# Streaming encoder: attention values held stationary in two column halves, whole key tiles

## What is computed

```
s = q @ k.T * HD**-0.5                      # fox: + c_q - c_k (running sums of a log forget value)
s = where(key allowed for query, s, -inf)   # fox: causal; dsa: chunk-causal and among the top 256 of an index score
p = softmax(s); o = p @ v                   # dsa: one k and one v for all four heads
```

## Time and profile before

| | us |
|---|---|
| median of 3 runs | 2261.97 (2259.77 to 2267.71) |
| the profiled execution's own time | 2242.35 |
| its span in the profile | 2240.4 |
| attention stage, layer 1 (from the keys' second turn to the mixers' first matmul) | 556.6 to 840.8 |
| TensorE busy in the span | 2069.9 (92%) |
| VectorE / ScalarE / GpSimd busy | 1483.6 / 641.7 / 325.3 |

### The profile page before, as it was taken

One profiled execution on the slowest core, in us unless ns is written; L12 is line 12 of the kernel. 1 busy time (PEld: TensorE's weight loads), 2 busy tenths in 40 slices (PEclk: granted clock), 3 DMA queues, 4 the chain that ended last, 5 costly groups with the idle time before them and its releaser, 6 DMA issues. The chain is left out here.

```text
span 2240.4 us, 27372 instructions
## 1 busy us (share of the span) xinstructions
PE 2069.9 (92%) x9906; PEld 1273.2 (57%) x9930; DVE 1483.6 (66%) x3125; ACT 641.7 (29%) x1478; POOL 325.3 (15%) x418
## 2 busy tenths in 40 slices
PE   3999999998999996999969999999989999979997
PEld 3644444446776775666445444444467777756663
DVE  3256999999454545877333579999975545468871
ACT  3334000101333333444143430011023333334441
POOL 0000000000000004656200000000000000146651
PEclk9999999999999996999979999999989999879999
DMA  7221132222102202233051212311130022022321
GB/s 278 81 68 35 67 118 75 75 68 72 33 8 88 81 1 104 69 104 108 38 187 53 66 67 83 108 65 59 58 80 20 6 92 76 32 74 76 118 87 59
DMA packets 144006, 169.95 MB, mean 76 GB/s; under 512 B 68560, under 2 KB 106192, under 8 KB 143600
## 3 DMA queue, kind: packets, MB, share of 16 engines
q1 hardware_dynamic: 118400, 135.52, 19.0%
q10 hardware_dynamic: 25472, 32.66, 4.1%
HBM read 115.53 MB, written 62.50 MB: 79 GB/s over the span
## 5 line engine op out<-in xcount | busy, mean ns | idle before, releaser
L767 PE MATMUL ps<-wring,xnT_arena 128*128 128x512 f32 (+3 forms) x2304 | 883.0, 540 | 0.0
L767 PEld LDWEIGHTS ps<-wring,xnT_arena 128*128 128x128 f32 x2304 | 430.7, 190 | 431.4 <-issue 369.4
L1485 DVE TENSOR_SCALAR_CACHE_REDUCE arena<-arena,theta 32x1056 bf16<-32x1056 f32 x496 | 471.5, 987 | 8.8
L1573 DVE TENSOR_REDUCE small<-ps 128x1 f32<-128x192 f32 (+9 forms) x148 | 114.0, 770 | 152.1 <-PE ps L942 145.4
L1178 ACT COPY arena<-ps 128x512 f32<-128x512 f32 (+2 forms) x96 | 51.2, 533 | 464.4 <-PE ps L767 464.4
L1470 DVE SCALAR_TENSOR_TENSOR arena<-arena,iw 128x512 f32<-128x512 f32 (+6 forms) x224 | 135.7, 606 | 57.3 <-ACT arena L1233 50.5
L1065 PEld LDWEIGHTS ps<-arena 128*128 128x128 f32 x632 | 102.6, 209 | 102.5 <-DVE arena L1673 51.7
L1065 PE MATMUL ps<-arena 128*128 128x128 f32 (+1 forms) x632 | 124.7, 330 | 38.9 <-DVE arena L1673 32.5
L1009 PE MATMUL ps<-wring,arena 128*128 128x512 f32 x320 | 152.6, 607 | 5.7 <-DVE arena L1614 5.7
L1326 ACT ACTIVATE arena<-ps,small 128x192 f32<-128x192 f32 (+9 forms) x148 | 111.0, 750 | 156.6 <-DVE small L1573 156.5
L1009 PE MATMUL ps<-wring,xnT_arena 128*128 128x512 f32 x256 | 118.3, 593 | 0.0
(11 more groups left out here) (239 smaller groups left out, 2526.0 us busy)
## 6 DMA issues: line engine op xcount, KB each, us to landing
wring<-in_w_in SPq DMA_DIRECT2D x24, 1024.0 KB, 7.6
projected<-arena ACTq DMA_DIRECT2D x96, 256.0 KB, 2.0
arena<-residual SPq DMA_DIRECT2D x36, 512.0 KB, 5.2
arena<-projected SPq DMA_DIRECT2D x36, 384.0 KB, 3.8
arena<-projected SPq DMA_DIRECT2D x18, 512.0 KB, 6.2
residual<-arena SPq DMA_DIRECT2D x18, 512.0 KB, 2.7
wring<-in_w_out SPq DMA_DIRECT2D x8, 1024.0 KB, 7.4
out<-arena SPq DMA_DIRECT2D x16, 512.0 KB, 3.9
```

The lines of the kernel that those rows point to most:

```text
L767: o = mm(bank(pbank(k), 0, wide), xnT[:, c, t * P:(t + 1) * P], w, start=(c == 0), stop=(c == CH - 1))
L1485: V.tensor_scalar(cmp_out[r, (i % 2) * WMAX:(i % 2) * WMAX + uw[u]], score[u][r], th_, 0.0, op, ALU.add, accum_out=into[r, i:i + 1]).then_ ...
L1573: V.tensor_reduce(mneg[:, s:s + 1], ps[:, base + lo:base + hi], X, ALU.max, negate=True).then_inc(a_max, 1)
```

## The change

Three things change together, all in the attention.

1. **Whole key tiles.** Key tile 0 is kept with all its 128 columns, and every piece is 128 wide and begins at a multiple of 128, scores at column 0 of the job's first bank. What has to stay hidden in tile 0 is hidden by a key row of -1e30 (in `negc` for fox, in row 64 of `dsaKT` for dsa), so `nometa` goes; `dsaown` goes from tiles 2 up, since `pen` now holds it. `pen` gets the 64 columns of tile 0's second half: VectorE writes it in two pieces and a memset.
2. **Values stationary.** `values` takes two heads at once: per key tile one matmul for the even head into partitions 0 to 63 and one for the odd head into 64 to 127 of bank 7, stationary the head's 64 value columns, moving its 128 turned exponentials. For tiles 4 up the work is cut into two halves along the keys. The result stands turned: ScalarE copies it to `OT`, TensorE turns it back into bank 6 (`turn_back`), VectorE scales both heads at once.
3. **The plan.** A pair's values can start only when both heads are turned; they are put in a queue `pvs` and taken at most one piece per job, after the next exponential. Four `ptile` buffers instead of two (`("L", h % 2)` for tiles 4 up, `("S", h % 2)` below). Bank 6 is now shared by the preps and the results turned back, so they wait for each other.

```diff
+PVK = [(m, u, i) for m in ("fox", "dsa") for group in UNIT_GROUPS for i in (range(2) if group != ["s"] else [0]) for u in group]
 def pieces_of(mu):
-            return [(0, HALF, 512 - HALF)] + [(HALF + P * j, P, 512 + P * j) for j in range(u)]
+            return [(P * j, P, P * j) for j in range(u + 1)]
 def plan_attend():
+            def values_now():
+                key, lo, hi = pvs.pop(0)
+                seq.append(("pv", (key, lo, hi)))
+                if hi == len(pieces_of(key[:2])):
+                    backs.append(key)
+                had, backs[:] = list(backs), []
                 if job != mine[-1]:
                     seq.append(("score", AJ[n + 1]))
                 if job == mine[-1]:
                     seq += [("prep", a) for a in now]
-                seq.append(("turn", job))
-                if job != mine[-1]:
-                    seq += [("prep", a) for a in now]
+                while pvs and (pvs[0][1] > 0 or any(ptile_of((k[0], k[1], 2 * k[2] + e)) == ptile_of(job) for k, _, _ in pvs for e in range(2))):
+                    values_now()
+                seq += [("back", key) for key in had] + [("turn", job)] + [("finish", key) for key in had]
...
                     seq.append(("exp", AJ[n + 1]))
-                if n > 0:
-                    seq.append(("pv", AJ[n - 1]))
+                if pvs:
+                    values_now()
+                if job != mine[-1]:
+                    seq += [("prep", a) for a in now]
+                elif job[2] % 2 == 1:
+                    half = (nb + 1) // 2 if job[1] >= 4 else nb
+                    pvs += [(pair_of(job), a, b) for a, b in ((0, half), (half, nb)) if a < b]
 def prepare(a):
+                        if back_then_prep.get(a) is not None:
+                            pe.wait_ge(a_o, a_o_at[back_then_prep[a]])
 def scores(m, u, h):
-                                    own = {"fox": "foxmeta", "dsa": "dsameta"}[m] if u == 0 else "nometa"
-                                    adds.append((CB("identb"), CB(own), 0, HALF))
-                                if u > 0 and key + w == width(u):
+                                    own = {"fox": "foxmeta", "dsa": "dsameta"}[m]
+                                    if u == 0:
+                                        adds.append((CB("identb"), CB(own), 0, HALF))
+                                if u > 0 and key + w == key_width(u) and (m == "fox" or u == 1):
 def values(key, lo, hi):
-                                v = foxV[0:w, i, h * HD:(h + 1) * HD] if m == "fox" else dsaKV[0:w, i, HD:2 * HD]
-                                o = mm(ps[:, o0:o0 + HD], pt, v, start=(i == 0), stop=(i == len(ch) - 1), skip_group_check=True)
+                                for e, job in enumerate(jobs_):
+                                    h = job[2]
+                                    v = foxV[:, b, h * HD:(h + 1) * HD] if m == "fox" else dsaKV[:, b, HD:2 * HD]
+                                    o = mm(ps[HD * e:HD * e + HD, o0:o0 + P], v, ptile[ptile_of(job)][:, P * b:P * b + P], start=first, stop=last, skip_group_check=True)
+def turn_back(key):
+                        pe.wait_ge(a_ot, a_ot_at[key])
+                        if k >= 1:
+                            pe.wait_ge(a_o, a_o_at[OTK[k - 1]])
+                        last_ = prep_then_back[key]
...
+                        tr(bank(6, 0, P), OT[k % 2], C("ident")).then_inc(a_bk, 1)
 # ScalarE
+                    def copy_out(key):
+                        act.wait_ge(a_pv, a_pv_at[key])
...
+                        nc.scalar.copy(OT[k % 2], bank(7, 0, P)).then_inc(a_ot, 1)
 # VectorE, penalties of a prompt tile
-                        o = V.tensor_scalar(pen[u][r], keep, 0.0, -BIG, ALU.is_equal, ALU.mult)
+                            V.tensor_scalar(pen[u][:, 0:HALF], keep[:, 0:HALF], 0.0, -BIG, ALU.is_equal, ALU.mult).then_inc(dve_own, one_more(own))
+                            V.memset(pen[u][:, HALF:P], 0.0).then_inc(dve_own, one_more(own))
+                            if u > 2:
+                                dve.wait_ge(dve_own, own[0])
+                            o = V.tensor_scalar(pen[u][:, P:penw[u]], keep[:, HALF:w], 0.0, -BIG, ALU.is_equal, ALU.mult)
 # VectorE, finish of a pair
+                            V.reciprocal(rinv[:, n:n + 2], rsum[:, n:n + 2]).then_inc(dve_own, one_more(own))
+                            dve.wait_ge(a_bk, a_bk_at[key])
+                            V.tensor_tensor(o_bc[r, u, c0 + P * i:c0 + P * i + P].rearrange("p (e d) -> p e d", e=2),
+                                            bank(6, 0, P)[r].rearrange("p (e d) -> p e d", e=2),
+                                            rinv[r, n:n + 2][:, :, None].broadcast_to([r.stop - r.start, 2, HD]), ALU.mult).then_inc(a_o, 1)
```

More of the change, by code:

```diff
@@ L63, in width, with key_width @@
     return HALF + P * t
+def key_width(t):
+    return P + P * t
 SW = PAST + NS
@@ L253, in encoder @@
         ca = carve(xnT_arena, CH * NT * P)
-        foxKT = ca([H, WMAX])
+        foxKT = ca([H, WK])
         foxV = ca([NT, H * HD])
-        ptile = [ca([NT * P]) for _ in range(2)]
+        ptile_long = [ca([NT * P]) for _ in range(2)]
+        ptile = {("L", i): ptile_long[i] for i in range(2)}
+        ptile.update({("S", i): ptile_short[i] for i in range(2)})
         pbuf = relu
-        cn_at = sum(uw.values()) + 2 * WMAX
+        cn_at = sum(uw.values()) + 2 * WK
         stage_at = cn_at + NT * NIX + WMAX + NS + SW + 2 * NI * P + 4 * D
@@ L483, in encoder @@
         before = {a: ([b for b in preps[:preps.index(a)] if tbank[b] == tbank[a]] or [None])[-1] for a in preps}
+        prep_then_back, back_then_prep, last_prep, last_back = {}, {}, None, None
+        for what, key in PLAN:
+            if what == "prep" and tbank[key] == 6:
+                back_then_prep[key], last_prep = last_back, key
+            elif what == "back" and key[1] != "s":
+                prep_then_back[key], last_back = last_prep, key
         attend_end = {e: sem(f"attend_end_{e}") for e in "ADP"}
@@ L992, in _ @@
                             values(*key)
+                        elif what == "back":
+                            turn_back(key)
                     pe.wait_ge(attend_end["A"], 1)
@@ L1335, in _ @@
                             exp(*key)
+                            for k in done:
+                                copy_out(k)
+                            done = []
+                        elif what == "pv":
+                            if key[0][1] != "s" and key[2] == len(pieces_of(key[0][:2])):
+                                done.append(key[0])
+                        elif what == "back":
+                            for k in done:
+                                copy_out(k)
+                            done = []
                         elif what == "turn":
```

172 lines of the change are left out of this document (115 added, 57 removed).

## The result

| | before | after |
|---|---|---|
| median (runs) | 2260.87 (4) | 2296.13 (2294.35 to 2301.28, 4) |
| ratio | | 1.0152, 95% interval 1.0111 to 1.0192 |
| span of the profiled execution | 2240.4 | 2293.1 |
| attention, layer 1 | 284.20 | 298.14 |
| attention, layer 2 | 286.38 | 300.64 |

The kernel is slower by 35 us, between 25 and 43 by the interval. 2282 was forecast, 20.4 more than before.

A forecast was written before the change was run, and what follows sets the result against it. TensorE's stream was taken as the attention's bound, hiding waits the change would expose. Attention +4.6, penalties +2.0, forget-value steps +0.6 and clock +3 made +10.2 us per layer, +20.4 on 2261.97: 2282, range 2214 to 2320.

The forecast's parts named there:

- (a): Attention: scores wait for copies queued behind VectorE's maximum, so shorter steps save only 29.7 us per layer.
- (c): Attention: preps wait in bank 6 for VectorE's finish, +13.0 us per layer for 10 preps; other preps +4.0.
- TensorE's stream: Attention: shorter values and scores take some 51 us per layer off TensorE's work, if nothing else held it.
- (b): Last turn of each group idles behind the exponential: 8 places, 1.8 us more each, +14.7 per layer.
- The 4.0 for the other preps: Attention: other preps wait for ScalarE's copies as before, with less in front, +4.0 us per layer.
- (e): Before the keys' turn: added VectorE penalty instructions count in full, +2.0 us per layer; ScalarE's moved forget-value steps +0.6.
- (f): Attention: TensorE, idle more, may be granted 1.2 instead of 2.4 GHz: +3 us per layer, between 0 and 15.

The follow-up runs named there:

- e7: Kernel before plus only the whole key tiles, with values, plan and finish untouched: 2232.34 us, ratio 0.9864 to the kernel before.
- e2: Changed kernel with ScalarE instead of VectorE copying the turned pieces of tiles 0 to 3: 2279.56 us, ratio 1.0055 to the kernel before.
- e5: Changed kernel multiplying only the first and last key tile of each values piece (computes something else): 2264.36 us, ratio 0.9995 to the kernel before.
- e1: Changed kernel with preps in groups of tiles 0 to 7 moved from bank 6 to another bank: 2284.62 us, ratio 1.0086 to the kernel before.
- e8: Changed kernel with e1, e2 and e3 together and each pair's values in one piece: 2275.07 us, ratio 1.0031 to the kernel before.
- e3: Changed kernel with ready values issued before the turn in a group's last job, not after it: 2292.62 us, ratio 1.0136 to the kernel before.

## Why the prediction was right, and where it was off

The sign and the range held, and so did the mechanism: the values' stream is about halved, and waits that it had covered come to light and cost more than it gives. The time grew by 35 where 20.4 was forecast. Two of the signs that I had named came out beyond their bounds: the attention is 298 long where 286 to 295 was said, and TensorE is busy 240 where 215 to 225 was said. That the total is as near as it is, is in part luck, since errors in (a) and (c) cancel.

- **TensorE's stream.** 51 less per layer was forecast; busy time fell by 33. The rest may be accounted for by the lower clock (16 us more of it, up to 8 us of work) and by busy time that the records show behind a last matmul before each idle time (an estimate: some 60 idle times of 0.17, since the record of a single turn back shows 0.28 where eight turns follow each other at 0.11). The split was wrong, though. I put 10 on the scores and 41 on the column halves; e7 shows 21 from the whole key tiles alone, 17 of them in the values. I had the entry into the 64-row shape at 0.09 per head, which the turns' 0.08 bears out, but the short first tile costs 0.24 more. The 0.12 per score that I took off in (a) is 0.05 in e7's step.
- **(a) Scores behind copies.** The floor of copies exists, e2 and the groups up to [2, 6] in e5 show it. The size failed: I had 6.58 for a step of [3, 7], and two large scores lie 6.97 and 7.86 apart (656.18, 663.15, 671.01), since a piece of values that stands before a turn delays that turn's copies, which I had counted only as filling. And [8], where I forecast 9.6 less in both mixers, is 5.6 longer in fox and 0.6 longer in dsa. In fox it has 6.9 us at the lower clock, up to 3.4 of the 5.6. It also has the preps in pairs through bank 6 and values forced before turns by the two `ptile` buffers; e1, e2 and e8 leave these preps where they are, and [8] stays at 31.7, 31.6 and 33.3. Which of these weighs most wasn't tried.
- **(b) The last turn of a group.** 14.7 forecast as added, 14.9 in all in the waits, up to 2.00 at tile 7. Right, though e3 shows that it isn't simply won back.
- **(c) Bank 6.** 13.0 forecast for 10 preps. The waits were 7.6 at 7 of them, and taking them out (e1) won 6.2 in waits. Right in kind, and about twice too large. The 9.9 and 9.4 of e1 hold a gain of the clock too. The 4.0 for the other preps was not measured by itself.
- **(e) Penalties.** The idle before the keys grew from 7.98 to 10.45 by TensorE's own rows, 2.5 against 2.0 forecast. A part of it is that the short tensor_scalar of 64 columns, 0.18 elsewhere, took 2.02 beside GpSimd's memset of 2.01: 1.84 more, where in the kernel before another instruction took 1.17 more beside it, so 0.7 of the 2.5.
- **(f) Clock.** 3 us per layer were forecast, by two or three pieces at the lower clock. It was 16 us more at that clock, up to 8 us of work.

Stage by stage: 7.6 was forecast for the attention (4.6 and 3), and 13.9 came. The clock accounts for up to 5 of the missing 6. (c) came out some 7 smaller than forecast, so (a), in which [8] is the largest part, must have saved some 8 less than its 29.7 (an estimate from the sum, with the untried terms as forecast). What I did not see at all is that the change holds a gain and a loss. With the whole key tiles alone the kernel is 29 us faster; the pairs' order, the column halves and the way back give 64 us away.

## What to carry to other kernels

A change that shortens one engine's stream is worth what is left after the stream's second job, covering other engines' chains. Count the cover at each job, not in sum: the same matmuls took 268 us with a piece behind every turn and 321 when bunched by pairs, with the waits and the lower clock that came with it. When a change has parts that can be made alone, price and run them alone; here the small part was the gain. And before two kinds of work share a PSUM bank, ask whose queue the release stands in.

## What the runs showed of the hardware

- A stationary operand with 64 rows at the head of a run with 128 rows costs 0.24 us per head in values of 8 tiles (1.97 against 1.73) and of 4 (1.08 against 0.84), though its matmul streams the same 64 columns. The Trainium skill, "TensorEngine Tiling (Array Packing)", Key Properties, says that a change of the tiling mode drains TensorE. The rows agree in that such a change costs time, at this price; a drain itself is in no row.
- The granted clock fell in the stage behind idle times that I had thought harmless: 2.00 at 675.60, 1.96 at 703.07, 1.00 at 728.38. It did not behind 1.87 at 645.03, so the length of one idle time does not tell. In all 23.5 us of 298 in layer 1 ran at the lower level.
- A VectorE instruction of 0.18 us took 2.02 us (at 546.92) while GpSimd's memset of 2.01 us ran (546.89). In the kernel before, another one (L1523, at 546.34) took 1.95 beside that memset; in the changed kernel it comes after the memset (550.70) and takes 0.78.
